# A two-block transformer layer: where the last gate, up and down products of both feed-forwards stand

## The reference, cut to what matters

```
u = rmsnorm(h, ffn_pre_norm)                    # block 1
gate, up = split(u @ w_gate_up)                 # 1024 -> 2 * 2816
y = (silu(gate) * up) @ w_down                  # 2816 -> 1024
h = h + rmsnorm(y, ffn_post_norm)
h = h + (p @ ple_proj) * sigmoid(h @ ple_gate)  # embedding gate 1

g = h @ w_gate                                  # block 2: gate goes through
conv = conv_b + sum_j shift(g, j) * conv_w[j]   # a causal convolution of width 3
h = h + (silu(conv) * (h_normed @ w_up)) @ w_down
h = h + sigmoid(rmsnorm(h) @ w_ple_gate) * (p_2 @ w_ple_proj)
```

## Time and the profile before

| | us |
|---|---|
| median of 3 runs | 3203.74 |
| lowest, highest | 3198.62, 3207.62 |
| profiled execution, its own time | 3198.64 |
| its span, first to last instruction | 3197.0 |
| first feed-forward, first split product to last down product | about 801 to 1504 |
| second feed-forward | about 2390 to 3094 |
| mean granted TensorE clock | 0.963 |

### The profile page before, as it was taken

One profiled execution on the slowest core, in us unless ns is written; L12 is line 12 of the kernel. 1 busy time (PEld: TensorE's weight loads), 2 busy tenths in 40 slices (PEclk: granted clock), 3 DMA queues, 4 the chain that ended last, 5 costly groups with the idle time before them and its releaser, 6 DMA issues.

```text
span 3197.0 us, 35161 instructions
## 1 busy us (share of the span) xinstructions
PE 2996.3 (94%) x14780; PEld 2497.9 (78%) x14780; DVE 1572.8 (49%) x1986; ACT 1018.6 (32%) x1377; POOL 118.1 (4%) x66
## 2 busy tenths in 40 slices
PE   8999988997999999999999888788999999999998
PEld 6878867886788888887778766677878888888877
DVE  4266766525434443445641377556435454444454
ACT  3144445433211111113331356756422111121131
POOL 0012211022000000000100000000000000000000
PEclk9999998998999999999999988888999999999999
DMA  4111220122111111111131100000211111111122
GB/s 158 53 40 53 74 80 1 42 91 86 66 47 53 40 53 53 47 46 40 46 98 48 33 14 23 1 1 1 95 32 58 48 47 53 46 50 50 45 81 79
DMA packets 45805, 165.59 MB, mean 52 GB/s; under 512 B 5424, under 2 KB 5936, under 8 KB 45648
## 3 DMA queue, kind: packets, MB, share of 16 engines
q1 hardware_dynamic: 45648, 163.34, 15.5%
HBM read 142.09 MB, written 21.23 MB: 51 GB/s over the span
## 4 chain that ended last, share of the span: by engine, by line
PE 86%; DVE 7%; ACT 4%; issue 2%; DMA 0%; SPq 0%; ACTq 0%; DVEq 0%
PE PS L274 22%; PE PS L276 22%; PE PS L278 22%; PE PS L476 2%; PE PS L478 2%; PE PS L477 2%; PE PS L1184 2%; PE PS L699 2%; PE PS L2647 1%; PE PS L2204 1%; PE PS L1154 1%; PE PS L1169 1%; PE PS L2172 1%; DVE w_lo L268 1%; DVE mla_small L2703 1%
## 5 line engine op out<-in xcount | busy, mean ns | idle before, releaser
L274 PE MATMUL PS<-u_hi_f,w_hi 128*128 128x512 f32 x1408 | 440.8, 395 | 27.5 <-DVE u_lo_f L395 15.1
L276 PE MATMUL PS<-u_lo_f,w_hi 128*128 128x512 f32 x1408 | 437.6, 392 | 0.0
L278 PE MATMUL PS<-u_hi_f,w_lo 128*128 128x512 f32 x1408 | 437.5, 392 | 0.0
L268 DVE TENSOR_TENSOR w_lo<-w_raw,w_hi 128x1024 fp32r<-128x1024 f32 x215 | 267.8, 1255 | 291.0 <-ACT w_hi L262 291.0
L262 ACT ACTIVATE w_hi<-w_raw 128x1024 fp32r<-128x1024 f32 x215 | 225.5, 1051 | 569.4 <-PE PS L278 429.5
L274 PEld LDWEIGHTS PS<-u_hi_f,w_hi 128*128 128x128 f32 x1408 | 266.7, 190 | 87.5 <-DVE w_lo L268 14.2
L276 PEld LDWEIGHTS PS<-u_lo_f,w_hi 128*128 128x128 f32 x1408 | 267.4, 190 | 56.3
L278 PEld LDWEIGHTS PS<-u_hi_f,w_lo 128*128 128x128 f32 x1408 | 266.9, 190 | 56.1
L274 PE MATMUL PS<-f_ah,w_hi 128*128 128x512 f32 x704 | 218.6, 392 | 10.2 <-DVE f_al L1687 10.2
L276 PE MATMUL PS<-f_al,w_hi 128*128 128x512 f32 x704 | 218.0, 391 | 0.0
L278 PE MATMUL PS<-f_ah,w_lo 128*128 128x512 f32 x704 | 217.9, 391 | 0.0
(11 more groups left out here) (381 smaller groups left out, 4979.6 us busy)
## 6 DMA issues: line engine op xcount, KB each, us to landing
w_raw<-in_weights SPq DMA_DIRECT2D x217, 512.0 KB, 3.6
H<-in_x_t SPq DMA_DIRECT2D x16, 512.0 KB, 4.4
stick_kept<-stick_stage SPq DMA_DIRECT2D x12, 512.0 KB, 2.9
mixer<-stick_kept SPq DMA_DIRECT2D x9, 512.0 KB, 6.8
p_kept<-p_stage SPq DMA_DIRECT2D x8, 512.0 KB, 4.0
h_kept<-H SPq DMA_DIRECT2D x8, 512.0 KB, 5.7
H<-h_kept SPq DMA_DIRECT2D x8, 512.0 KB, 7.1
p_pp<-p_kept SPq DMA_DIRECT2D x8, 512.0 KB, 6.0
```

The lines of the kernel that those rows point to most:

```text
L268: dve.tensor_tensor(self.w_lo[i][:], self.w_raw[i][:], self.w_hi[i][:].bitcast(F32), ALU.subtract).then_inc(*self.s("w_lo").up(g))
L274: ins = e.matmul(banks[i], lh, rh[i], start=first, stop=False)
L276: ins = e.matmul(banks[i], lh, rl[i], start=False, stop=False)
L278: ins = e.matmul(banks[i], ll, rh[i], start=False, stop=last)
```

## The change

In both feed-forwards, the down products of pair 9 (tiles 18 and 19) move from between gate 20 and up 20 to behind up 21. PE's order at the end becomes gate 20, up 20, gate 21, up 21, down of pair 9, down of pair 10. The weights in memory are laid in that order.

Since tiles 20 and 21 are then finished before pair 9's parts have been read, their parts get rooms of their own (`ah_last`, `al_last`). In the first feed-forward these are slots 49, 50 and, for tile 21, slots 26 and 27 (the first tiles of `u_hi_f`, which up 21 is the last to read); in the second 33, 41, 17 and 18. `p_raw` of the first embedding gate had slots 49 and 50; it moves to 34 and 35, which are `u_lo_f`, so its two loads move from near the start of the first feed-forward to behind up 21, after the load of unit base + 67.

In the last pair, the first four blocks go in the order (c, k) = (0,0), (1,0), (0,1), (1,1), so that the second unit of down weights is wanted two blocks later. ACT's splits of the two units that replace pair 9's weights move behind tile 21's work and behind `act_embeddings`; DVE's first one stands before the last addition of pair 9, its second one after it. `dve_embeddings` comes after both.

```
+        self.ah_last, self.al_last = ([[tile(f"f{n + 1}_{part}_last{j}", slots[n][j], dt=F32R) for j in range(2)]
+                                       for n in range(2)]
+                                      for part, slots in (("ah", ((49, 26), (33, 17))), ("al", ((50, 27), (41, 18)))))
...
-        self.p_raw = [[tile(f"p{n + 1}_raw{k}", (49, 44)[n] + k)[:] for k in range(2)] for n in range(2)]
+        self.p_raw = [[tile(f"p{n + 1}_raw{k}", (34, 44)[n] + k)[:] for k in range(2)] for n in range(2)]
...
-        for i in range(FF_TILES // 2 - 1):
+        for i in range(FF_TILES // 2 - 2):
...
-        downs[FF_TILES // 2 - 1] = base + 4 + 6 * (FF_TILES // 2 - 1)
+        at = base + 4 + 6 * (FF_TILES // 2 - 2)
+        for j in range(2):
+            gates[FF_TILES - 2 + j], ups[FF_TILES - 2 + j] = at + 2 * j, at + 2 * j + 1
+            downs[FF_TILES // 2 - 2 + j] = at + 4 + 2 * j
...
+    def ff_parts(self, n, t):
+
+        if t < FF_TILES - 2:
+            return self.ah[n][:, t % 2, :], self.al[n][:, t % 2, :]
+        return self.ah_last[n][t % 2][:], self.al_last[n][t % 2][:]
...
+        last = i == FF_TILES // 2 - 1
+        order = [(c, k) for c in range(KT) for k in range(2)]
+        if last:
+
+            order[0:4] = [(0, 0), (1, 0), (0, 1), (1, 1)]
+        for c, k in order:
+            p, w, cc = self.ff_down_pair(i, c), (g + k) % RING, self.chunk(c)
...
-            if t >= 2 and t % 2 == 0:
+            if t % 2 == 0 and t < FF_TILES - 2:
                 self.pe_down(n, t // 2 - 1, downs[t // 2 - 1])
             self.pe_product(ups[t], pu, U)
+        for i in range(FF_TILES // 2 - 2, FF_TILES // 2):
+            self.pe_down(n, i, downs[i])
         self.claim(3)
-        self.pe_down(n, FF_TILES // 2 - 1, downs[FF_TILES // 2 - 1])
...
         if n == 0:
             self.act_embeddings(0)
+        for j in range(2):
+            self.act_split(downs[i - 1] + j + RING)
...
+            if i == FF_TILES // 2 - 2 and c == KT - 1:
+                self.dve_split(g + RING)
...
         i = FF_TILES // 2 - 1
+        self.dve_down(n, i - 1, downs[i - 1])
+        self.dve_split(downs[i - 1] + 1 + RING)
         if n == 0:
             self.dve_embeddings(0)
         self.dve_down(n, i, downs[i])
...
-            if n == 0 and g == base + 2 * RING:
-                for i in range(5, KT):
-                    sp.wait_ge(*self.d(f"p2_stored{i % 3}").at(i))
+            if n == 0 and g == base + 67:
+                sp.wait_ge(*self.s("w_used").at(self.ff_units(0)[1][FF_TILES - 1]))
                 for k in range(2):
                     sp.dma_start(self.p_raw[0][k], self.a["p_t"][k]).then_inc(*self.d(f"tile_in{k}").up("p1"))
```

More of the change, by code:

```diff
@@ L1448, in pe_down @@
             pe.wait_ge(*self.s("f_al").at(n, 2 * i + j))
-        AH, AL = self.ah[n], self.al[n]
-        for c in range(KT):
-            p = self.ff_down_pair(i, c)
-            self.claim(p, dve=1)
-            for k in range(2):
-                w = (g + k) % RING
-                if c == 0:
-                    pe.wait_ge(*self.s("w_lo").at(g + k))
-                cc = self.chunk(c)
-                mm = self.mm3(self.halves(p), self.w_hi[w][:, cc], self.w_lo[w][:, cc],
-                              [AH[:, k, h * HALF:(h + 1) * HALF] for h in range(2)],
-                              [AL[:, k, h * HALF:(h + 1) * HALF] for h in range(2)], k == 0, k == 1)
-                if c == KT - 1:
-                    mm.then_inc(*self.s("w_used").up(g + k))
-            if c < KT - 1:
+        last = i == FF_TILES // 2 - 1
[4 more added lines that the diff above has]
+            p, w, cc = self.ff_down_pair(i, c), (g + k) % RING, self.chunk(c)
+            ah, al = self.ff_parts(n, 2 * i + k)
+            if k == 0:
+                self.claim(p, dve=1)
+            if c == 0:
+                pe.wait_ge(*self.s("w_lo").at(g + k))
+            mm = self.mm3(self.halves(p), self.w_hi[w][:, cc], self.w_lo[w][:, cc],
+                          [ah[:, h * HALF:(h + 1) * HALF] for h in range(2)],
+                          [al[:, h * HALF:(h + 1) * HALF] for h in range(2)], k == 0, k == 1)
+            if c == KT - 1:
+                mm.then_inc(*self.s("w_used").up(g + k))
+            elif k:
                 mm.then_inc(*self.s("f_down").up(n, i, c))
@@ L1577, in act_ffn @@
             self.act_split(gates[t] + RING)
-            if t >= 2 and t % 2 == 0:
+            if t >= 2 and t % 2 == 0 and t < FF_TILES - 2:
                 for j in range(2):
@@ L1581, in act_ffn @@
             act.wait_ge(*self.s("f_gated").at(n, t))
-            if t >= 2:
+            if 2 <= t < FF_TILES - 2:
                 act.wait_ge(*self.s("w_used").at(downs[t // 2 - 1] + 1))
-            act.activation(self.ah[n][:, t % 2, :], prod[:], ACT.Copy).then_inc(*self.s("f_ah").up(n, t))
+            act.activation(self.ff_parts(n, t)[0], prod[:], ACT.Copy).then_inc(*self.s("f_ah").up(n, t))
             self.act_split(ups[t] + RING)
@@ L1588, in act_ffn @@
             self.act_embeddings(0)
+        for j in range(2):
+            self.act_split(downs[i - 1] + j + RING)
+        if n == 0:
             q = [sg, prod]
@@ L1686, in dve_ffn @@
                     dve.wait_ge(*self.d(f"p2_stored{i % 3}").at(i))
-            dve.tensor_tensor(self.al[n][:, t % 2, :], prod[:], self.ah[n][:, t % 2, :].bitcast(F32),
-                              ALU.subtract).then_inc(*self.s("f_al").up(n, t))
+            ah, al = self.ff_parts(n, t)
+            dve.tensor_tensor(al, prod[:], ah.bitcast(F32), ALU.subtract).then_inc(*self.s("f_al").up(n, t))
             self.dve_split(ups[t] + RING)
         i = FF_TILES // 2 - 1
+        self.dve_down(n, i - 1, downs[i - 1])
+        self.dve_split(downs[i - 1] + 1 + RING)
         if n == 0:
@@ L2882, in ffn @@
         for g in range(n):
-            if g:
-                u += chan(gate, 2 * g * P)
+            u += chan(gate, 2 * g * P)
+            if 0 < g < n - 1:
                 u += rows(down, 2 * g - 2) + rows(down, 2 * g - 1)
-            else:
-                u += chan(gate, 0)
             u += chan(up, 2 * g * P) + chan(gate, (2 * g + 1) * P) + chan(up, (2 * g + 1) * P)
-        return u + rows(down, 2 * n - 2) + rows(down, 2 * n - 1)
+        for k in range(2 * n - 4, 2 * n):
+            u += rows(down, k)
+        return u
     w1 = np.asarray(inp["w_in"])[0]
```

## The result

| | before | changed |
|---|---|---|
| median of six runs, us | 3203.59 | 3187.95 |
| lowest, highest | 3198.62, 3207.62 | 3183.07, 3188.64 |
| ratio, with 95% interval | | 0.9949 (0.9939 to 0.9959) |
| profiled execution: time, span | 3198.64, 3197.0 | 3187.80, 3186.4 |

The changed kernel is 0.51% faster by the ratio; 0.46% and 3189.2 us were forecast. By medians it is 15.6 us (0.49%).

The account below looks back on a forecast made before the run. PE was taken to bound the kernel, busy 94% of the span. The sum 0 - 10.50 - 4.08 = -14.58 us, counted from the median of 3203.74, gave 3189.2 us, with a range from 3181 to 3198.

Parts of the forecast that it names:

- The gap: Behind up 21 in each feed-forward, PE waits 5.25 us for tile 21's low part; all 10.50 us would go.
- The slow matmuls behind it: Last down of each feed-forward runs partly at the lower clock; 1.66 and 2.42 us, 4.08 together, would go.
- The slacks: Behind up 21 (its end is T), splits and DVE's queue stay 1.5 and 1.0 us ahead of PE; cost 0.
- p_raw: Its two loads, moved behind up 21 (ends at T), land at T + 14, bounds T + 10.7 and T + 26.0; cost 0.
- rival 4: p_raw lands late, delaying PE past T + 20.1 (T: up 21's end); slower by over 9.6 us; chance 0.02.
- p_pp: Second feed-forward: its six loads are issued later, near T + 23 (T: up 21's end), still before use; cost 0.
- Rival 1: The 10.50 us of idle go, but slow-clock stretches turn up elsewhere; time 3193.2 us, chance 0.12.
- The signs named ahead: Changed profile: no f_al wait, 43.5 us unbroken behind up 21, feed-forward ends 6.9 and 14.6 us earlier.
- The base: Sum gives 3184.1 us against the profiled execution's 3198.64; counted from the runs' median, 5.10 higher, 3189.2 us.

Follow-up runs that it names:

- the filled gap: Kernel before, with 14 further matmuls, results unread, in PE's gap behind up 21 of both feed-forwards; 0.9988 to before, median 3198.09 us.
- praw_end: Changed kernel with the two p_raw loads issued later, behind the first unit of pair 9's down; 0.9968 to before, median 3193.64 us.
- the halves: The change made in one feed-forward only, against before: first alone 0.9969, 3192.13 us; second alone 0.9988, 3198.51 us.
- second_only: Kernel before with the change in the second feed-forward alone, p_raw loaded where before loads it; 0.9988 to before, median 3198.51 us.
- plain_order: Changed kernel with the last pair's first four blocks in plain order, (0,0), (0,1), (1,0), (1,1); 0.9960 to before, median 3190.39 us.
- early_split: Changed kernel with up 1's weights split ahead of the statistics at the start of both feed-forwards; 0.9925 to before, median 3178.43 us.
- three_splits: Changed kernel with weight splits ahead of the statistics in both feed-forwards and the second embedding gate; 0.9907 to before, median 3173.81 us.
- shift5: Changed kernel with 5 further matmuls, results unread, between the last two downs of the second feed-forward; one execution, 3183.57 us.

## Why the prediction was right, point by point

**The gap.** 5.25 us at each end, 10.50 together: exactly gone. The two ends last 76.16 us each, three products and four down units (two downs) of 10.88 us each, 7 x 10.88, without a stop.

**The slow matmuls behind it.** 1.66 and 2.42 were taken from the length of the last downs; the ends shortened by 6.91 and 7.67, and the filled gap shortened them by 1.65 and 2.42 by itself.

**The slacks.** Worked out for the low part of the last pair's second unit: T + 23.0, measured T + 22.98. The embedding parts on DVE: T + 27.7, measured T + 27.5 (1483.76 + 2.35 = 1486.11). The first addition of the last pair: T + 28.9, measured T + 28.6. No wait of PE in 43.52 us. The prediction named the new order of four blocks as what saves the second unit (slack of 1.5 with it). Without it there was 0.14 left, and it cost 0.05.

**`p_raw`.** T + 14 was taken, T + 12.5 measured, well within the bounds of T + 10.7 and T + 26.0. The threshold in rival 4 was a microsecond too early, T + 20.1 for T + 21.1, since only ACT's second part waits for the second load. Its mechanism is shown by praw_end.

**`p_pp`.** The six loads go out from 3060.6 on, and the first use is at 3117.7, 57 us later. No cost.

**Rival 1**, that the clock's part is given back elsewhere, was the nearest to the truth and was priced wrongly. It had 4.08 us come back. In fact 2.86 came back in one stretch and 3.42 more were gained in another, both mostly by the clock; that the moment of the waits decides this is likely and not shown, and nothing in the runs points to a sum that has to be paid back. That the total came to the forecast within 1.2 us rests partly on these two nearly cancelling: the halves alone brought 10.0 and 3.6 us, not 6.9 and 7.7. The prediction's argument against this rival, that nothing is given back where PE doesn't stand, holds, but PE does stand in the last stretch, for 3.06 us, and the prediction did not look at what that wait would cost at another moment.

**The signs named ahead.** Two of them fail as they were written. The end of the first feed-forward was to come 6.9 us earlier than 1504.49 and that of the second 14.6 earlier than 3094.19; they came at 1502.12 and 3080.73, 2.4 and 13.5 earlier, because the changed kernel's execution was 4.5 us behind by the end of gate 20 (and 3.4 us quicker between the feed-forwards). The gain is seen only in the length of each end. ACT's first embedding part started at T + 10.97, at the edge of the T + 11 that was named.

**The base.** The sum was made against the profiled execution and then counted from the median of the runs, 5.10 us higher. That was right: before's profiled execution had been lucky ahead of 780 us, and the difference of the two profiled spans, 10.6, would have misled. Three more runs of before moved its median only from 3203.74 to 3203.59.

## What to carry to other kernels

When PE waits for the last part of a chain through DVE and ACT at the end of a loop, look for a block of its own work whose inputs have long been ready and put it behind the last producer; the price is rooms for the parts that now live longer, and the loads that had those rooms. Size the gain as idle time plus the excess length of the work behind the gap, which the distance of starts gives directly. A gain of a few microseconds shifts all that follows, and each remaining wait of about 3 us on PE could here cost up to 2.9 us more or less, so compare stretches and not only totals, and remove those waits too.

## What the runs showed of the hardware

A wait of PE of 3.05 or 3.06 us, the same in eleven traces, has between 0.14 us (before) and 2.88 us (changed kernel) of slow matmuls behind it, with 1.53 and 1.73 in between. Waits of 3.48 to 3.53 us cost 0.13 to 0.18 (such as the changed kernel's), about 1.7 (before, second_only, plain_order) or 2.7 (early_split, three_splits). The Trainium skill says, on the page "TensorE: Matmul & The Clock Gate", section "Part 1: The HAM clock gate (the "warmup" mystery)", that the moment at which activity lifts the clock varies from run to run. The traces agree: shift5 and the changed kernel run the same program between the two feed-forwards and take 1504.13 and 1502.45 us for it. Whether moving the work within the program changes that moment as well could not be told apart from it.

The clock can also fall after PE has begun again: in shift5 rows start 0.57 and 0.46 us apart behind the wait, and then 0.85 (3118.39 to 3120.87).

Matmuls whose results nobody reads kept the clock up: with 14 of them (3.5 us) in a gap of 5.25 us, and a wait of 1.32 us left, the work behind ran at 1.00.
